# Reordering weight panels around a TensorE-bound head loop: gMLP inputs first, up-projections inside the last head, and two changes of consumption order

## The reference

```python
# first block
h = rmsnorm(x, norm_mix)
zu, zv, zq, zf, zi, zo, g_a, g_b = split(h @ w_in)     # widths 512, 512, then six of 1024
y_a = (gelu(zu) * (W_s @ layernorm(gelu(zv)) + b_s)) @ w_up_a            # gMLP branch
# HGRN2 branch, 8 heads of 128: log_f = log_sigmoid(zf), k = sigmoid(-zf), q = silu(zq)
#   S_t = diag(f_t) S_{t-1} + k_t v_t^T,  o_t = S_t^T q_t
y_b = (rmsnorm(o) * silu(zo)) @ w_up_b
x = x + (sigmoid(g_a) * y_a + sigmoid(g_b) * y_b) @ w_out
x = x + square(relu(rmsnorm(x) @ w_ff1)) @ w_ff2
x = rmsnorm(x, final_norm)
# second block: short convolution mixer (b * conv(c * h)) @ a_w_out, conv FFN,
#   then forgetting attention (16 heads of 64) and a second conv FFN
```

## Time and profile before

| | |
|---|---|
| time, median of 3 runs | 2070.67 us (2069.67 to 2070.74) |
| the profiled execution's own time | 2068.97 us |
| its span, first to last instruction | 2067.2 us |
| PE busy | 2043.3 us (99%), 9522 matmuls |
| DVE, ACT, POOL busy | 971.9, 782.7, 854.7 us (47%, 38%, 41%) |
| panels, DMA traffic | 353 panels, 194.28 MB, mean 94 GB/s |

### The profile page before, as it was taken

One profiled execution on the slowest core, in us unless ns is written; L12 is line 12 of the kernel. 1 busy time (PEld: TensorE's weight loads), 2 busy tenths in 40 slices (PEclk: granted clock), 3 DMA queues, 4 the chain that ended last, 5 costly groups with the idle time before them and its releaser, 6 DMA issues.

```text
span 2067.2 us, 23862 instructions
## 1 busy us (share of the span) xinstructions
PE 2043.3 (99%) x9522; PEld 1674.6 (81%) x9522; DVE 971.9 (47%) x1481; ACT 782.7 (38%) x1123; POOL 854.7 (41%) x357
## 2 busy tenths in 40 slices
PE   9899999999999999999999999999999999999999
PEld 6788888877888888888888888888877778888887
DVE  6688778524322213534454242454356645424242
ACT  5445544543322223612332222246366633222222
POOL 3333433454444444444444444454422234444444
PEclk9999999999999999999999999999999999999999
DMA  4222222242223232322323223232311112323323
GB/s 167 80 72 82 72 82 76 98 157 93 101 92 102 92 102 92 100 94 94 100 91 104 92 93 102 92 114 90 102 62 54 59 63 98 102 88 99 102 92 113
DMA packets 55119, 194.28 MB, mean 94 GB/s; under 512 B 6112, under 2 KB 6368, under 8 KB 55008
## 3 DMA queue, kind: packets, MB, share of 16 engines
q1 hardware_dynamic: 55008, 192.75, 28.4%
HBM read 190.62 MB, written 2.10 MB: 93 GB/s over the span
## 4 chain that ended last, share of the span: by engine, by line
PE 95%; DVE 3%; ACT 1%; issue 1%; DMA 0%; POOL 0%; SPq 0%; DVEq 0%; POOLq 0%
PE ps L1286 29%; PE ps L1288 29%; PE ps L1287 29%; PE ps L1392 1%; PE ps L1578 1%; PE ps L1611 1%; PE ps L1602 1%; PE ps L1541 1%; PE ps L1543 1%; PE ps L1542 1%; PE ps L1294 1%; DVE arena L911 0%; DVE arena L750 0%; PE ps L1378 0%; PE ps L1414 0%
## 5 line engine op out<-in xcount | busy, mean ns | idle before, releaser
L354 POOL TENSOR_TENSOR w_lo<-w_raw,w_hi 128x1024 fp32r<-128x1024 f32 x353 | 854.5, 2424 | 1200.4 <-ACT w_hi L371 1195.8
L1286 PE MATMUL ps<-a_hi,w_hi 128*128 128x512 f32 x1472 | 582.3, 396 | 10.0 <-DVE a_lo L768 4.7
L1288 PE MATMUL ps<-a_hi,w_lo 128*128 128x512 f32 x1472 | 573.7, 390 | 0.0
L1287 PE MATMUL ps<-a_lo,w_hi 128*128 128x512 f32 x1472 | 573.5, 390 | 0.0
L371 ACT CAST w_hi<-w_raw 128x1024 fp32r<-128x1024 f32 x353 | 366.6, 1042 | 357.4 <-PE ps L1288 320.8
L1286 PE MATMUL ps<-b_hi,w_hi 128*128 128x512 f32 x1176 | 460.5, 392 | 4.1 <-POOL w_lo L354 4.1
L1287 PE MATMUL ps<-b_lo,w_hi 128*128 128x512 f32 x1176 | 458.6, 390 | 0.0
L1288 PE MATMUL ps<-b_hi,w_lo 128*128 128x512 f32 x1176 | 458.6, 390 | 0.0
L739 DVE TENSOR_TENSOR arena<-ps,inv_rms 128x512 f32<-128x512 f32 x200 | 138.0, 690 | 442.4 <-PE ps L1288 422.6
L1286 PEld LDWEIGHTS ps<-a_hi,w_hi 128*128 128x128 f32 x1472 | 276.5, 188 | 71.1 <-issue 11.0
L1287 PEld LDWEIGHTS ps<-a_lo,w_hi 128*128 128x128 f32 x1472 | 276.5, 188 | 57.9 <-issue 2.4
(11 more groups left out here) (192 smaller groups left out, 1619.1 us busy)
## 6 DMA issues: line engine op xcount, KB each, us to landing
w_raw<-in_panels SPq DMA_DIRECT2D x353, 512.0 KB, 3.5
x<-in_xT SPq DMA_DIRECT2D x16, 256.0 KB, 2.7
outT<-x SPq DMA_DIRECT2D x8, 256.0 KB, 2.0
consts<-in_const SPq DMA_DIRECT2D x1, 528.5 KB, 8.0
arena<-in_rows SPq DMA_DIRECT2D x1, 256.0 KB, 4.2
arena<-in_ws SPq DMA_DIRECT2D x1, 256.0 KB, 4.7
consts<-in_late SPq DMA_DIRECT2D x1, 168.0 KB, 2.7
params<-in_param SPq DMA_DIRECT2D x1, 116.0 KB, 2.0
```

The lines of the kernel that those rows point to most:

```text
L354: nc.gpsimd.tensor_tensor(w_lo[:, p % RING, :], w_raw[:, p % RING, :], w_hi[:, p % RING, :].bitcast(F), ALU.subtract).then_inc(w_low, 1)
L1286: nc.tensor.matmul(o, wh, hi[:, kt, :], start=(kt == 0), stop=False)
L1287: nc.tensor.matmul(o, wh, lo[:, kt, :], start=False, stop=False)
L1288: ins = nc.tensor.matmul(o, wl, hi[:, kt, :], start=False, stop=(kt == tiles - 1))
```

## The change

- `ORDER`: `zv` 0 to 3, `zu` 0 to 3, then eight heads with two fill panels each (`ga` 0 to 7 in heads 0 to 3, `gb` 0 to 7 in heads 4 to 7), then `upa` 0 to 7.
- The gMLP's transposes, statistics, layer norm, `mix` and `gmlp_out` stand ahead of head 0, among the `zu` panels. So do the four `gelu(zu)`, which stood in head 1.
- The eight `sigmoid(ga)` move from the last head's part into head 7, ahead of its second log-sigmoid, with a `load_exp_and_log()` behind them.
- `last_head` runs head 7's products between the eight `upa` panels alone.
- `upb`/`out1`: ACT splits `y[m]` and DVE makes its low half panel by panel.
- `out2`: input tiles 0 to 6 of panels 0 and 1 first, then tile 7 of both.

```diff
-FILL = {0: [("zu", i) for i in range(4)], 8: [("gb", 6), ("gb", 7), ("upa", 0), ("upa", 1), ("upa", 2)]}
...
+FILL = [[("ga" if _i < DT else "gb", _i % DT) for _i in (2 * _h, 2 * _h + 1)] for _h in range(HEADS_H)]
+ORDER = [("zv", i) for i in range(GROUPS)] + [("zu", i) for i in range(GROUPS)]
+for _h in range(HEADS_H):
+    ORDER += [("heads", 4 * _h + i) for i in range(4)] + FILL[_h]
+ORDER += [("upa", i) for i in range(DT)]
# ACT, ahead of head 0
+            high(6)
+            load_exp_and_log()
+            high(7)
...
+            norm_gmlp()
+            high(8)
+            gelu(zu[:, 0, :], ("zu", 0))
+            gelu(zu[:, 1, :], ("zu", 1))
+            high(9)
+            gelu(zu[:, 2, :], ("zu", 2))
+            gelu(zu[:, 3, :], ("zu", 3))
# ACT, head: sigmoid(ga) in head 7
                 high(p + 3)
-                if h is None:
+                if h == HEADS_H - 1:
                     for m in range(DT):
+                        act.wait_ge(evicted, AT["ga", m] + 1)
                         nc.scalar.activation(y[:, m, :], y[:, m, :], ACT.Sigmoid).then_inc(gate_a, 1)
+                    load_exp_and_log()
# ACT, behind head 7
+            def last_head(a):
+                p = S["upa"]
+                high(p + 2)
+                copy_turned(a)
+                act.wait_ge(o_arg, a + 1)
+                nc.scalar.activation(z_o[:, :], z_o[:, :], ACT.Exp).then_inc(o_sig, 1)
+                for n in range(3, 8):
+                    high(p + n)
+                square_output(a)
+                high(p + 8)
+                root(R_HEAD + a, ps[:, 2, :], 1.0 / P, o_inv[:, :])
+                high(p + 9)
+                split_output(a)
...
+            sigmoid_b(0)
+            act.wait_ge(made, AT["gb", 7] + 1)
+            for m in range(DT):
                 high(S["upb"] + m + 2)
-            for m in range(DT):
-
+                if m < DT - 1:
+                    sigmoid_b(m + 1)
                 act.wait_ge(y_mixed, m + 1)
...
                 split(a_hi[:, m, :], y[:, m, :]).then_inc(hid_high, 1)
# DVE, last head
+            def last_head(a):
+                p = S["upa"]
+                take_levels(0, a)
+                squash_output(a)
+                fill_out(p)
+                take_levels(1, a)
+                gate_output(a)
+                fill_out(p + 1)
+                fill_out(p + 2)
+                states(a)
+                fill_out(p + 3)
+                take_levels(2, a)
+                take_levels(3, a)
+                for n in range(4, 7):
+                    fill_out(p + n)
+                norm_output(a)
+                fill_out(p + 7)
# DVE, ahead of head 0
+            fill_out(S["zu"])
+            gmlp_stats()
+            fill_out(S["zu"] + 1)
+            dve.wait_ge(ln_rooted, 1)
+            for b in range(BLK):
+                layer_norm(b)
+            gmlp_bias()
+            fill_out(S["zu"] + 2)
+            fill_out(S["zu"] + 3)
+            for gr in range(GROUPS):
+                gmlp_out(gr)
# DVE, upb
-            for m in range(DT):
-                low_hid(HID_MIX + m + 1, m, y[:, m, :], A)
+                if m > 0:
+                    low_hid(HID_MIX + m, m - 1, y[:, m - 1, :], A)
+            low_hid(HID_MIX + DT, DT - 1, y[:, DT - 1, :], A)
# PE, last head
-                p = AT["gb", 6]
-                product(p, a_hi, a_lo)
+                up_a(0)
                 turns(a)
                 levels(0, a)
-                product(p + 1, a_hi, a_lo, part=(0, 4))
+                up_a(1)
                 levels(1, a)
-                product(p + 1, a_hi, a_lo, part=(4, DT))
+                up_a(2)
                 chunk_kv(a)
                 levels(2, a)
-                up_a(0)
+                up_a(3)
                 levels(3, a)
-                up_a(1)
+                up_a(4)
                 outputs(a)
-                up_a(2)
+                up_a(5)
+                up_a(6)
                 output_sums(a)
-                for m in range(3, DT):
-                    up_a(m)
-
+                up_a(7)
# PE, ahead of head 0
+            product(S["zu"], a_hi, a_lo)
+            for b in range(BLK):
+                turn_zv(b)
+            pe.wait_ge(ws_masked, 1)
+            nc.tensor.matmul(ps[:, 7, :], c("ones"), ws_sb[:, :, :], start=True, stop=True).then_inc(ws_summed, 1)
+            for m in range(1, GROUPS):
+                product(S["zu"] + m, a_hi, a_lo)
+            mix()
# PE, out2
-            linear(S["out2"], DT, a_hi, a_lo, hid_low, HID_CONV)
+
+            for part in ((0, 7), (7, DT)):
+                for m in range(2):
+                    product(S["out2"] + m, a_hi, a_lo, DT, hid_low, HID_CONV, part)
+            linear(S["out2"] + 2, DT - 2, a_hi, a_lo, None, None)
```

More of the change, by code:

```diff
@@ L445, in split_gmlp @@
                     split(gm_hi[:, gr, :], zu[:, gr, :]).then_inc(gm_high, 1)
+            norm_gmlp()
[5 more added lines that the diff above has]
+            gelu(zu[:, 3, :], ("zu", 3))
             def head(h, a):
-                p = AT["heads", 4 * h] if h is not None else AT["gb", 6]
+                p = AT["heads", 4 * h]
                 high(p + 2)
[L450 to L456, removed]
-                if a is not None:
[L458 to L470, removed]
+                act.wait_ge(evicted, p + 1)
+                log_sigmoid_part(za[:, :], z[:, :], f_log)
+                if a is not None:
+                    copy_turned(a)
+                act.wait_ge(f_k, h + 1)
+                if a is not None:
+                    act.wait_ge(diag_made, a + 1)
+                nc.scalar.activation(even(k), even(za), ACT.Exp)
+                nc.scalar.activation(odd(k), odd_back(za), ACT.Exp).then_inc(k_done, 1)
                 if a is not None:
@@ L492, in head @@
                     split_gmlp((0, 1) if h == 3 else (2, 3))
[L493 to L495 removed]
+                act.wait_ge(spans_done, h * 3 + 2)
+                nc.scalar.activation(qk[:, 2:6, :], qk[:, 2:6, :], ACT.Exp).then_inc(decays_done, 1)
                 if a is not None:
[L497 to L498 removed]
@@ L499, in head @@
[L499 to L505 removed]
+                    square_output(a)
+                act.wait_ge(spans_done, h * 3 + 3)
@@ L514, in head, with copy_turned @@
+                log_sigmoid_part(z_o[:, :], silu_o[:, h % 2, :], o_log)
                 if a is not None:
-                    act.wait_ge(y_b, a + 1)
-                    split(b_hi[:, a, :], o_tmp[:, :]).then_inc(hid_high, 1)
-                for e in range(1, len(fill)):
-                    high(p + 6 + e)
+                    split_output(a)
+                high(p + 7)
+            def copy_turned(a):
+                act.wait_ge(turned_v, a + 1)
+                nc.scalar.copy(v_nat[:, :, :], ps[:, 2, :].rearrange("p (b n) -> p b n", b=BLK)).then_inc(copied_v, 1)
+                act.wait_ge(turned_k, a + 1)
+                nc.scalar.copy(k_nat[:, :, :], ps[:, 3, 0:384].rearrange("p (b n) -> p b n", b=BLK - 1)).then_inc(copied_k, 1)
@@ L940, in head @@
+            def head(h, a):
+                p = AT["heads", 4 * h]
+                if a is not None:
+                    dve.wait_ge(q_done, h)
+                scale_out(z[:, :], p).then_inc(evicted, 1)
+                if a is not None:
                     take_levels(0, a)
+                    dve.wait_ge(cum_done, h)
+                dve.wait_ge(f_log, h + 1)
+                link(v.scalar_tensor_tensor(g[:, :], z[:, :], 0.0, za[:, :], ALU.min, ALU.subtract))
+                v.tensor_tensor(za[:, :], g[:, :], z[:, :], ALU.subtract).then_inc(f_k, 1)
@@ new lines, in head @@
+                wait_made(p + 2)
+                v.tensor_tensor(even(vT), even(bank(p + 2)), even(inv_rms), ALU.mult)
+                v.tensor_tensor(odd(vT), odd_back(bank(p + 2)), odd_back(inv_rms), ALU.mult).then_inc(evicted, 1)
+                span(3)
+                span(4).then_inc(spans_done, 1)
+                for n in range(5, LEVELS):
+                    span(n)
+                span(LEVELS).then_inc(spans_done, 1)
+                scale_out(silu_o[:, h % 2, :], p + 3).then_inc(evicted, 1)
@@ L1035, in _ @@
                 head(h, h - 1 if h > 0 else None)
-            head(None, HEADS_H - 1)
-            for m in range(3, DT):
-                fill_out(S["upa"] + m)
+            last_head(HEADS_H - 1)
             for m in range(DT):
@@ L1429, in head @@
                 product(p, a_hi, a_lo)
-                if h == 0:
-                    for b in range(BLK):
-                        turn_zv(b)
-                    pe.wait_ge(ws_masked, 1)
-                    nc.tensor.matmul(ps[:, 7, :], c("ones"), ws_sb[:, :, :], start=True, stop=True).then_inc(ws_summed, 1)
                 if a is not None:
```

197 lines of the change are left out of this document (68 added, 129 removed).

## The result

The changed kernel takes 2059.27 us, median of 5 runs (2057.80 to 2062.56). The kernel before, timed beside it, takes 2070.74 (2069.67 to 2073.18). The ratio is 0.9941, with a 95% interval of 0.9930 to 0.9953: faster by 0.59%. The forecast was 2060.7 us and a gain of 10.0. The span shrank by 9.7 us, from 2067.2 to 2057.5.

The account below looks back on a forecast made before the run. PE bounds the kernel, busy 2043.3 of 2067.2 us, so only its waits can be won. Terms -0.14 + 3.66 - 0.2 + 1.77 + 4.18 + 0.76 gave 10.0 us, forecasting 2060.7 us, range 2057.5 to 2064.5.

Parts of the forecast that it names:

- Nearly all of the idle time: Claim that most of PE's some 24 us idle sits in eight places, from head 0 to behind out3.
- no idle over 0.5 then until out3: Sign on PE's timeline: after head 0's idles near 2 and 0.3 us, none above 0.5 before out3.
- Ahead of head 0: `zu` stretch before head 0: same work in another order, costed at nothing; 2.6 us if cover for table loads were gone.
- Head 0: Three PE waits: first 2.0 against 1.86 us (loss 0.14), second stays 0.50, third goes (gain 3.66).
- rival A: Head 0: POOL's backlog still catches L911, PE waits 7.2 us, gain only 2.8, time 2067.9; chance 0.08.
- Last head: Wait among the up-projections goes, gain 1.77 us; 0.2 allowed for what comes close here and in head 7.
- rival B: Up-projections wait for DVE or POOL because POOL's port holds DVE; price some 3 us, time 2063.7; chance 0.12.
- out1 and out2: Low-half waits at the start of out1 go, gain 4.18 us; out2's 1.20 wait goes, net gain 0.76.
- Head 7: Eight sigmoids and two table loads delay the log-sigmoid 1.05 us; 0.29 slack left, cost 0, at worst 1.05.
- The allowance of 0.2: Loss of 0.2 us allowed for close slacks in the last head and head 7.
- Rival C: Behind out3: PE's clock fall to 1.2 GHz, about 2.5 us, stays away, time 2058.2; chance 0.08.
- Rival D: Heads 1 to 7: head 0's lag of 2.0 + 0.5 us returns in each, time 2078.2; chance 0.04.

Follow-up runs that it names:

- Experiment 5: Changed kernel with four more VectorE operations (results not used) in head 0 ahead of the seven L925; span 2066.5 us against 2057.5.
- Experiment 3: Changed kernel with the last head's weights for `upb` 0 and 1 cast only behind the split of the head's output; span 2061.7 us against 2057.5.
- experiment 1: Changed kernel with out1's splits and low halves put back behind the last `upb` panel; 2064.98 us, ratio 0.9967 to the kernel before.
- experiment 2: Changed kernel with out2 multiplied panel by panel, as before; one execution, span 2057.0 us against 2057.5.
- experiment 4: Changed kernel with three more ScalarE copies (results not used) ahead of head 7's eight sigmoids; one execution, span 2058.7 us against 2057.5.
- experiment 9: Changed kernel with out3's fourth weight panel cast early and its second panel added right behind the first; 2056.07 us, ratio 0.9924 to the kernel before.
- `best`: Changed kernel with out3's early cast and early add, head 0's evictions earlier and head 1's first weights cast earlier; 2053.85 us, ratio 0.9913 to the kernel before.
- `early_evict`: Changed kernel with head 0's value and output-gate panels taken out of PSUM earlier by VectorE; one execution, span 2060.2 us against 2057.5.
- `out3_early`: Changed kernel with out3's fourth weight panel cast as soon as its first panel is finished; 2057.98 us, ratio 0.9942 to the kernel before.
- experiments 8: Changed kernel with out3's fourth weight panel cast early, the same run as `out3_early`; 2057.98 us, ratio 0.9942 to the kernel before.

## Why the prediction was right

- **What bounds the kernel.** Right: TensorE's work is 2043.1 us as before, and the span fell by what its waits lost. "Nearly all of the idle time" in eight places was too much said. They add up to 15.6 of 23.9 us. The rest lies in the first 29 us and behind the last matmul, out of the change's reach, and 0.61 at 1519.30. This last one stands unchanged in the new kernel (0.63), so the sign "no idle over 0.5 then until out3" was put wrongly.
- **Ahead of head 0.** Costed at nothing, and right: between 28.89 and 87.03 TensorE waits for nothing.
- **Head 0.** First wait forecast at 2.0 in all, measured 1.78 plus 0.24. Second unchanged, 0.26. Third gone. Experiment 5 shows its cause and its price for rival A (7.04 for 7.2), so A was a real danger, at a margin of 0.29. One reading was wrong and cost nothing: that each of the seven but the first waited for one of GpSimd's operations. Three did, and four did not.
- **Last head.** Gone, with nothing in its place, so rival B's wait did not come. Its cause did, twice: L944 took the 1.08 us shown above, in GpSimd's shadow as L958 had in the earlier trace rows, and L782, which the prediction lists as L768, was held to 2.12 us. It ended at 416.79, 1.6 ahead of the matmul that wants it (tile 7 of `upb` 0, at 418.43), so slack covered it. Experiment 3 shows ScalarE's order as the cause of such a wait.
- **out1 and out2.** 4.18 and 0.76 as forecast by the rows of experiments 1 and 2. What was missing is a term: a wait may bring the clock down too, and then costs more than its length plus 0.24. In experiment 1 the two waits and their 0.24 come to 3.6 us of the 6.4 lost; the other 2.8 is what the matmuls at 1.2 GHz took longer. In the two traces on which the forecast and the result rest the clock stayed up at out1, so the term was zero there, and one trace of a kernel could not have shown that.
- **Head 7.** No wait, as forecast. The list of what stands behind the log-sigmoid lacked `take_levels(3)` and through it `outputs` (experiment 4).
- **The sum.** 10.0 against 9.7 in span. The allowance of 0.2 was not needed. The first products started 0.3 later (11.01, 10.72 before), and at out3 TensorE ran 0.7 us longer at 1.2 GHz (1664.21 to 1669.8 after, 1674.25 to 1679.1 before), which costs about 0.4: 10.0 + 0.2 - 0.3 - 0.4 = 9.5.
- **Rival C.** Its fall did not stay away by itself. With a wait of 2.26 it did in one trace (experiment 9), but not in the other (`best`, 2.27).
- **Rival D.** No wait in heads 1 to 7.
- **The medians.** The timed runs gained 11.5, more than the span's 9.7. Rows explain the 9.7. The rest is within the spread of either kernel's runs, so that the median came out 1.4 from the forecast speaks neither for it nor against it.

## What to carry to other kernels

When one engine is busy 99% of the time, list each of its waits with its releaser and the neighbours' order there, and price the change wait by wait. Then ask of each what is late next: twice here it took back most of the gain (`early_evict`: 1.69 of idle came for 2.04 that went; `out3_early`: 3.90 for 4.06). An engine's operations that share a port with another's should be placed by where the other's series begins, not by their own length. And where single executions are compared, compare the way between two matmuls on either side of the edit, not the span.

## What the runs showed of the hardware

- Idle stretches of TensorE bring its clock down in some executions and not in others. The two waits at out1 (2.20 and then 1.50 or 0.96) left the clock up in the trace of before and brought it to 1.2 GHz in experiment 1. Behind the wait of about 4 us at out3 it fell in each of the eleven traces that have it, and with 2.26 it stayed up in one trace and fell in another (`best`). The wait of 2.77 in the attention stage took it down in `early_evict` and not in `best`. An idle of 3.42 in head 0 of the kernel before left it up (granted 1.00 from 79 to 87). So in these traces the length of one idle stretch does not decide it. The Trainium skill (TensorE: Matmul & The Clock Gate, "The HAM clock gate") says that the activity window runs freely and is not reset by the kernel. These rows agree, as far as the same wait brings the fall in one execution and not in another. That it explains the runs' spread (2068.9 to 2074.8 for the kernel before in one batch) is argued, since only profiled executions show the place of a fall. Of these runs, 2074.8 and 2074.3 had a mean granted clock of 0.996, but so had one of 2071.5, and the fastest 0.997. So the clock is not all of it.
- Who gets the port shared by VectorE and GpSimd is not settled by the start times in the trace. In the changed kernel's attention stage GpSimd's low half starts first, at 1508.12, and is the one held (3.23 us), while VectorE's L1175 at 1508.44 takes 0.68. In `early_evict` the two stand the same 0.32 us apart (1507.64 and 1507.96), and it went the other way. In `best` it did so once more (1505.76 and 1506.09, 2.82). The profile's starts on GpSimd may be rough, so what decides is not shown. The row of `early_evict`:

```profile
1507.96 2.82 DVE L1184 TENSOR_TENSOR gm_hi<-arena,gm_hi 128x512 fp32r<-128x512 f32 x1
```

  TensorE then waits 2.77 instead of 0.63 us. In a comparison by single executions this alone can outweigh the effect sought.
- A VectorE copy with one SBUF source was held as well (L770: 2.15 us in experiments 8 and 9; 0.43 to 0.53 for this operation in the changed kernel).
